# Kernel head of a hybrid mLSTM and gMLP step: four instead of six columns of x turned ahead of the first product, and lower halves made ahead of the next normalisation

## The chip, the cores and the metric

The kernel runs on one core of a Trainium2 chip. The metric is the device time of one execution in microseconds; three runs of the kernel before gave a median of 1468.02 us (1467.85 to 1468.49). The engines are PE (TensorE; its weight loads are listed as PEld), DVE (VectorE), ACT (ScalarE), POOL (GpSimd) and SP (which issues transfers). DMA queue q1 carries the transfers that SP issues, q0 those that POOL issues.

## The reference

One layer. `h = RMSNorm_pre(x)` for 256 prompt rows and 32 sample rows (288 in all), then one product `h @ w_in` whose columns feed two mixers: a chunkwise mLSTM (heads of 256) and a gMLP with a spatial gate. Their outputs are projected, gated and summed, multiplied by `w_out`, normalised and added to x. Only its first steps matter here:

```
h      = x * rsqrt(mean(x*x) + eps) * g_pre
proj   = h @ w_in                      # 2048 x (9 x 2048 + 16 + ...) columns
vb_n   = layernorm(vb)                 # vb: one of the column groups
s      = tril(w_s[g]) @ vb_n + b_s     # spatial gate; w_s is used transposed
y_b    = u * s * silu(zb)
```

## The kernel before

All large products are made in three matmuls. Each operand is split into an upper half (rounded to the fp32r format) and a lower half (the rest): `xh`, `xl` for the normalised x and `whi`, `wlo` for the weights. Then `xh*whi + xl*whi + xh*wlo` is summed (L454, L455, L456). The contraction runs over 16 blocks of 128 rows, k = 0 to 15, and each weight tile ("pair", 256 output columns) comes in four chunks c of four k each. There are 104 pairs; pairs 0 to 7 make `vb`. Per k and pair there are two column halves, so six matmuls of 128x288.

A chunk of weights goes round this ring: SP loads it into `raw` (L394), ACT rounds it into `whi` (L805), DVE subtracts to give `wlo` (L1070), and PE uses both. SP may load the next pair's chunk c into `raw` once DVE has made the lower half of this pair's chunk c. ACT may write `whi` for the next pair's chunk once PE has finished with this pair's.

The head, with all its order written by hand: x is loaded and squared (ACT and DVE), POOL makes the reciprocal root (L1675), and ACT (prompt rows 0 to 127, L830) and DVE (the other rows, L1099) normalise it in quarters of 512 columns, that is four k at a time: `normalise(0)` serves k = 0 to 3, `normalise(1)` k = 4 to 7 and so on. PE turns each k with three transposes (L488, L489: function `turn_x`), ACT writes `xh` from the turned block (L840) and DVE writes `xl` (L1112). Then PE can make the product of that k. Before the first product PE fills time with matmuls nobody reads (L470).

In the head PE turns k = 0 to 5, then goes into the first pair: in front of product k it turns block k + 5 (for k = 1 to 10) and waits for `xl` of k (function `x_piece`). So all 16 blocks are turned when product k = 10 begins. DVE normalises quarter 1 before its first `xl`, and quarters 2 and 3 in front of `xl` of k = 4 and 6.

What hangs on the last turned block (semaphore `x_t` = 16): POOL waits for it (L1683), since the normalised x makes room for its next tiles. It sets a few tiles and then issues four loads of 3 MB together, in this order: `wsn` (the gate weights, L1694), `bsb`, `lng` and `lnb` (L1698). PE turns `wsn` after chunk 0 of pair 1 (L505), DVE masks it into `wsT` (L1200), right behind the lower half of pair 2's chunk 0, and PE reads `wsT` after chunk 2 of pair 1 (L512, function `w_s_corners`):

```
    def w_s_corners():
        pe.wait_ge(ws_set, 2)
        nc.tensor.matmul(ps[:, 6, 0:S], rep4[:], wsT[:, :, 0:TS], start=True, stop=True)...
```

Between pairs 0 and 1 PE makes the gate columns from 32 matmuls (L497, L498) with a small tile `wg2` that ACT and DVE split right after the last `xh` and `xl`; ACT then makes `whi` of pair 1's chunks 0 to 2.

Of the kernel before, what the change touches and what calls it, by code (L numbers as in the profile page):

```python
# [102 lines left out]
def build(nc, x_prompt, x_sample, state_C, state_n, state_m, state_conv, g_pre, w_in, b_ig, b_fg,  # L103
# [258 lines left out]
    def x_bank(k):  # L362
        return 2 + k % 6
# [77 lines left out]
    def _(pe):  # L441
# [26 lines left out]
        def idle_run(n):  # L468
            for _ in range(n):
                nc.tensor.matmul(ps[:, 7, 0:P], ident[:], ident[:], start=True, stop=True)  # L470
# [6 lines left out]
        def turn_x(k0, k1):  # L477

            for k in range(k0, k1):
                if k % 4 == 0:  # L480
                    pe.wait_ge(x_norm_a, k // 4 + 1)
                    pe.wait_ge(x_norm, 2 * (k // 4) + 2)
                if k == 4:
                    pe.wait_ge(par_set, 1)
                if k >= 6:
                    pe.wait_ge(x_lo, k - 5)
                for t in range(2):
                    pe.transpose(ps[:, x_bank(k), P * t:P * t + P], hb0[:, t, P * k:P * k + P], ident[:])  # L488
                pe.transpose(ps[:, x_bank(k), TP:TP + P], hb0[:, 2, P * k:P * k + P],  # L489
                             ident[:]).then_inc(x_t, 1)  # L490
# [47 lines left out]

        def x_piece(k):

            if 1 <= k <= 10:
                turn_x(k + 5, k + 6)
            pe.wait_ge(x_lo, k + 1)

        def v_body(i, first=False, second=False):
            for s in range(2):
                for c in range(CHUNKS):
                    chunk(V0 + s + 2 * i, c, s, None if first else i, xh, xl,
                          x_piece if first and s == 0 else None)
                    if first and (s, c) == (0, 3):  # L550
                        gate_sums()
                    if first and (s, c) == (1, 0):
                        turn_w_s()
                    if c == 1 and not (first and s == 0):
                        if first:
                            pe.wait_ge(g_in, 1)
                        if second and s == 0:
                            pe.wait_ge(ws_set, 3)
                        if not (first or second):
                            pe.wait_ge(g_set, 1)  # L560
                        turn_v(1 - s, 2 * i + s - 1, reused=not (first or second and s == 0))
                    if first and (s, c) == (1, 2):
                        w_s_corners()
                    if second and (s, c) == (1, 3):
                        pe.wait_ge(tok_ev, 3)
                        gates()

        idle_run(11)
        turn_x(0, 6)
        v_body(0, first=True)  # L570
        v_body(1, second=True)
        with pe.Fori(2, 4) as i:
# [493 lines left out]
    def _(dve):  # L1066
        def split_lo(pair, c):

            dve.wait_ge(hi_ready, 4 * pair + c + 1)
            nc.vector.tensor_tensor(wlo[:, c], raw[:, c], whi[:, c].bitcast(F32),  # L1070
                                    ALU.subtract).then_inc(lo_ready, 1)
# [24 lines left out]
        def normalise(q):  # L1096
            for t in (1, 2):
                n = P if t < 2 else S
                nc.vector.tensor_scalar(hb0[0:n, t, QUARTERS[q]], xt[0:n, t, QUARTERS[q]], rstd[0:n, t:t + 1], None,  # L1099
                                        ALU.mult).then_inc(x_norm, 1)  # L1100

        normalise(0)
        split_lo(0, 0)
        normalise(1)
        dve.wait_ge(par_set, 1)
        for k in range(KT):
            if k in (4, 6):
                normalise(k // 2)
            if k in (4, 8, 12):
                split_lo(0, k // CK)  # L1110
            dve.wait_ge(x_hi, k + 1)
            nc.vector.scalar_tensor_tensor(xl[:, k, :], ps[:, x_bank(k), 0:T], par1[:, 32 + k:33 + k],  # L1112
                                           xh[:, k, :].bitcast(F32), ALU.mult, ALU.subtract).then_inc(x_lo, 1)
# [719 lines left out]
```

## Time and profile before

| | us |
|---|---|
| median of three runs | 1468.02 |
| the profiled execution, its own time | 1468.24 |
| its span, first to last instruction | 1465.8 |
| PE busy | 1451.2 (99%) |
| DVE busy | 866.5 (59%) |
| ACT busy | 618.7 (42%) |
| POOL busy | 189.0 (13%) |

The mean granted TensorE clock is 0.997 of full speed. A table of stages of the head, from the view that cuts the span into stretches (busy us of each engine, granted clock, share of the DMA engines):

| stretch, us | PE | DVE | ACT | POOL | clock | DMA |
|---|---|---|---|---|---|---|
| 10 to 13 | 3.00 | 2.38 | 2.51 | 2.04 | 1.00 | 1.09 |
| 16 to 20 | 4.00 | 4.00 | 4.00 | 0.00 | 1.00 | 0.54 |
| 24 to 28 | 4.00 | 2.96 | 2.34 | 0.33 | 1.00 | 0.62 |
| 36 to 44 | 8.00 | 2.60 | 0.99 | 0.00 | 1.00 | 1.02 |
| 44 to 52 | 8.00 | 7.43 | 5.19 | 0.00 | 1.00 | 0.75 |

A busy PE in this table only says that its queue of matmuls never ran dry; how fast it goes is read from the distance between the starts of its matmuls. The engine that waits is found by the bracket behind a row of the timeline, which names the idle time in front of the row and what ended it.

### The profile page before, as it was taken

To read this page: it belongs to the slowest core of one execution; us is meant where nothing else is said; L and a number is where in the kernel's file an instruction comes from. 1 tells how busy PE (TensorE), PEld (TensorE's weight loads), DVE (VectorE), ACT (ScalarE), POOL (GpSimd) and SP (SyncE) were. 2 spreads that over 40 slices of the span, in tenths; PEclk is the share of its full clock that TensorE was granted. 3 is DMA by queue.
4 is the path that set the end of the run, shared out by engine and by line. 5 is a ranking of instruction groups with operands and counts; after the bars stand their busy time and mean duration, and the time that the engine had idled before them with its cause. 6 is when DMAs were issued, how large, how long until landed. Compare 5 with 4: busy or idle time off the path is not lost. (4 is left out here: it accounts for less than half of the span.)

```text
span 1465.8 us, 31006 instructions
## 1 busy us (share of the span) xinstructions
PE 1451.2 (99%) x11100; PEld 1430.1 (98%) x11100; DVE 866.5 (59%) x1433; ACT 618.7 (42%) x870; POOL 189.0 (13%) x340
## 2 busy tenths in 40 slices
PE   9999999999999999999999999999999999999996
PEld 9999999999999999999999999999999999999996
DVE  7766555564434447586767676767667544545444
ACT  6433343343333334454544444545454433333442
POOL 4000000001000000404040414141312000000000
PEclk9999999999999999999999999999999999999998
DMA  7664655557555568696959596979696665555543
GB/s 229 224 160 136 182 162 166 162 151 242 185 172 174 182 185 212 168 298 170 311 161 311 164 303 173 289 185 294 174 295 161 217 180 176 177 178 188 172 159 140
DMA packets 310676, 292.11 MB, mean 199 GB/s; under 512 B 82880, under 2 KB 297608, under 8 KB 309840
## 3 DMA queue, kind: packets, MB, share of 16 engines
q1 hardware_dynamic: 291424, 243.05, 58.4%
q0 software_dynamic: 18960, 48.48, 9.7%
q8 instruction: 23, 0.38, 0.1%
q10 hardware_dynamic: 256, 0.10, 0.0%
q14 instruction: 13, 0.11, 0.0%
HBM read 266.11 MB, written 25.44 MB: 199 GB/s over the span
## 5 line engine op out<-in xcount | busy, mean ns | idle before, releaser
L1070 DVE TENSOR_TENSOR wlo<-raw,whi 128x1024 fp32r<-128x1024 f32 x416 | 506.6, 1222 | 518.2 <-ACT whi L805 516.3
L454 PE MATMUL ps<-xh,whi 128*128 128x288 f32 x2560 | 761.2, 297 | 0.0
L455 PE MATMUL ps<-xl,whi 128*128 128x288 f32 x2560 | 757.6, 296 | 0.0
L456 PE MATMUL ps<-xh,wlo 128*128 128x288 f32 x2560 | 754.6, 295 | 0.0
L805 ACT ACTIVATE whi<-raw 128x1024 fp32r<-128x1024 f32 x416 | 439.3, 1058 | 690.8 <-PE ps L456 655.2
L454 PEld LDWEIGHTS ps<-xh,whi 128*128 128x128 f32 x2560 | 481.7, 188 | 4.8 <-issue 3.3
L455 PEld LDWEIGHTS ps<-xl,whi 128*128 128x128 f32 x2560 | 481.3, 188 | 0.4
L456 PEld LDWEIGHTS ps<-xh,wlo 128*128 128x128 f32 x2560 | 481.0, 188 | 0.0
L455 PE MATMUL ps<-yl,whi 128*128 128x288 f32 x512 | 151.6, 296 | 0.0
L456 PE MATMUL ps<-yh,wlo 128*128 128x288 f32 x512 | 151.0, 295 | 0.0
L454 PE MATMUL ps<-yh,whi 128*128 128x288 f32 x512 | 150.1, 293 | 0.0
L454 PEld LDWEIGHTS ps<-yh,whi 128*128 128x128 f32 x512 | 96.4, 188 | 0.0
L455 PEld LDWEIGHTS ps<-yl,whi 128*128 128x128 f32 x512 | 96.2, 188 | 0.0
L456 PEld LDWEIGHTS ps<-yh,wlo 128*128 128x128 f32 x512 | 96.2, 188 | 0.0
L454 PE MATMUL ps<-mh,whi 128*128 128x288 f32 x248 | 73.5, 297 | 0.0
L455 PE MATMUL ps<-ml,whi 128*128 128x288 f32 x248 | 73.4, 296 | 0.0
L456 PE MATMUL ps<-mh,wlo 128*128 128x288 f32 x248 | 73.1, 295 | 0.0
L1756 POOL DMA_DIRECT2D out_dram<-cst x64 | 36.0, 562 | 229.3 <-DVE cst L1450 224.3
L454 PEld LDWEIGHTS ps<-mh,whi 128*128 128x128 f32 x248 | 46.6, 188 | 0.0
L455 PEld LDWEIGHTS ps<-ml,whi 128*128 128x128 f32 x248 | 46.6, 188 | 0.0
L456 PEld LDWEIGHTS ps<-mh,wlo 128*128 128x128 f32 x248 | 46.6, 188 | 0.0
L1351 DVE SCALAR_TENSOR_TENSOR hb<-xp,par,hb 128x312 f32<-128x312 f32 x96 | 46.3, 537 | 0.0
(348 smaller groups left out, 1014.8 us busy)
## 6 DMA issues: line engine op xcount, KB each, us to landing
raw<-in_w_in_dram SPq DMA_DIRECT2D x320, 512.0 KB, 3.9
raw<-in_w_pb_dram SPq DMA_DIRECT2D x32, 512.0 KB, 3.4
Cin<-in_state_mlstm_C_dram POOLq DMA_DIRECT2D x16, 1024.0 KB, 8.6
Xb<-in_state_mlstm_C_dram SPq DMA_DIRECT2D x256, 64.0 KB, 3.7
out_dram<-Cin POOLq DMA_DIRECT2D x16, 1024.0 KB, 6.3
raw<-in_w_pa_dram SPq DMA_DIRECT2D x32, 512.0 KB, 3.4
raw<-in_w_out_dram SPq DMA_DIRECT2D x32, 512.0 KB, 3.5
bcs<-rows_d POOLq DMA_DIRECT2D x8, 304.0 KB, 3.8
```

What stands on the lines that cost most here:

```text
L454: nc.tensor.matmul(out, whi[:, c, kk, cols], mh_[:, k, :], start=(k == 0), stop=False)
L455: nc.tensor.matmul(out, whi[:, c, kk, cols], ml_[:, k, :], start=False, stop=False)
L456: last = nc.tensor.matmul(out, wlo[:, c, kk, cols], mh_[:, k, :], start=False, stop=(k == KT - 1))
L805: nc.scalar.activation(whi[:, c], raw[:, c], ACT.Copy).then_inc(hi_ready, 1)
L1070: nc.vector.tensor_tensor(wlo[:, c], raw[:, c], whi[:, c].bitcast(F32), ALU.subtract).then_inc(lo_ready, 1)
L1351: ins = nc.vector.scalar_tensor_tensor(out, src, w_at, out, ALU.mult, ALU.add)
L1756: pool.dma_start(blocks_of(conv_p_v, h, s, g), cst[g:g + 3, 2 * s:2 * s + 2, :]).then_inc(cst_out, 16)
```

## The change

On PE, four blocks are turned ahead of the first product. Blocks 4 and 5 are turned in front of product k = 2, and block k + 3 in front of product k for k = 3 to 12. On DVE, `normalise(1)` moves from ahead of the loop to in front of `xl` of k = 2, and quarters 2 and 3 move from k = 4 and 6 to k = 5 and 8. ACT's, POOL's and SP's code is as it was; ACT still normalises quarter 1 ahead of its loop and quarters 2 and 3 at k = 4 and 6.

```diff
         def x_piece(k):
 
-            if 1 <= k <= 10:
-                turn_x(k + 5, k + 6)
+            if k == 2:
+                turn_x(4, 6)
+            if 3 <= k <= 12:
+                turn_x(k + 3, k + 4)
             pe.wait_ge(x_lo, k + 1)
...
         idle_run(11)
-        turn_x(0, 6)
+        turn_x(0, 4)
         v_body(0, first=True)
...
         normalise(0)
         split_lo(0, 0)
-        normalise(1)
         dve.wait_ge(par_set, 1)
         for k in range(KT):
-            if k in (4, 6):
-                normalise(k // 2)
+            if k in (2, 5, 8):
+                normalise((k + 1) // 3)
             if k in (4, 8, 12):
                 split_lo(0, k // CK)
             dve.wait_ge(x_hi, k + 1)
```

Line numbers in the changed kernel are larger by two from `x_piece` on, and by one behind DVE's loop.

First place: PE from the turning of block 3 on. `hb_77` is the normalised x (it shares a place with what lies there later). Before:

```order
L488 MATMUL ps<-ident,hb_77 128x128 x2
L489 MATMUL ps<-ident,hb_77 128x128
L488 MATMUL ps<-ident,hb_77 128x128 x2
L489 MATMUL ps<-ident,hb_77 128x128
L488 MATMUL ps<-ident,hb_77 128x128 x2
L489 MATMUL ps<-ident,hb_77 128x128
L454 MATMUL ps<-xh,whi 128x288
```

Now:

```order
L488 MATMUL ps<-ident,hb_77 128x128 x2
L489 MATMUL ps<-ident,hb_77 128x128
L454 MATMUL ps<-xh,whi 128x288
L455 MATMUL ps<-xl,whi 128x288
L456 MATMUL ps<-xh,wlo 128x288
```

Six transposes have left the place ahead of the first product; twelve matmuls, products k = 0 and 1, now stand ahead of them.

Second place: DVE from `normalise(0)` on. Before:

```order
L1099 TENSOR_SCALAR hb_77<-xt,rstd 128x512
L1099 TENSOR_SCALAR hb_77<-xt,rstd 32x512
L1070 TENSOR_TENSOR wlo<-raw,whi 128x1024
L1099 TENSOR_SCALAR hb_77<-xt,rstd 128x512
L1099 TENSOR_SCALAR hb_77<-xt,rstd 32x512
L1112 SCALAR_TENSOR_TENSOR xl<-ps,par_63,xh 128x288 x4
L1099 TENSOR_SCALAR hb_77<-xt,rstd 128x512
L1099 TENSOR_SCALAR hb_77<-xt,rstd 32x512
L1070 TENSOR_TENSOR wlo<-raw,whi 128x1024
```

Now:

```order
L1101 TENSOR_SCALAR hb_77<-xt,rstd 128x512
L1101 TENSOR_SCALAR hb_77<-xt,rstd 32x512
L1072 TENSOR_TENSOR wlo<-raw,whi 128x1024
L1113 SCALAR_TENSOR_TENSOR xl<-ps,par_63,xh 128x288 x2
L1101 TENSOR_SCALAR hb_77<-xt,rstd 128x512
L1101 TENSOR_SCALAR hb_77<-xt,rstd 32x512
L1113 SCALAR_TENSOR_TENSOR xl<-ps,par_63,xh 128x288 x2
L1072 TENSOR_TENSOR wlo<-raw,whi 128x1024
L1113 SCALAR_TENSOR_TENSOR xl<-ps,par_63,xh 128x288
```

Two `xl` now stand ahead of the pair of instructions that normalises quarter 1, and quarter 2 comes behind the lower half of weight chunk 1.

Third place: PE around the end of the turning, with its waits. Before, behind the last turned block, where product k = 11 has no turn in front of it:

```order
L488 MATMUL ps<-ident,hb_77 128x128 [waits x_lo]
L488 MATMUL ps<-ident,hb_77 128x128
L489 MATMUL ps<-ident,hb_77 128x128
L454 MATMUL ps<-xh,whi 128x288 [waits x_lo]
L455 MATMUL ps<-xl,whi 128x288
L456 MATMUL ps<-xh,wlo 128x288
L454 MATMUL ps<-xh,whi 128x288
L455 MATMUL ps<-xl,whi 128x288
L456 MATMUL ps<-xh,wlo 128x288
L454 MATMUL ps<-xh,whi 128x288 [waits x_lo]
```

Now the last turned block stands in front of product k = 12, the first of weight chunk 3, and waits for that chunk's lower half as well:

```order
L488 MATMUL ps<-ident,hb_77 128x128 [waits x_lo,lo_ready]
L488 MATMUL ps<-ident,hb_77 128x128
L489 MATMUL ps<-ident,hb_77 128x128
L454 MATMUL ps<-xh,whi 128x288 [waits x_lo]
L455 MATMUL ps<-xl,whi 128x288
```

The last turn has moved behind two more products.

## Rows read from the trace of the kernel before

**Rows 1.** The page: PE and its weight loads over the span.

```profile
PE 1451.2 (99%) x11100; PEld 1430.1 (98%) x11100; DVE 866.5 (59%) x1433; ACT 618.7 (42%) x870; POOL 189.0 (13%) x340
```

**Rows 2.** PE's waits over the span: total us, times, longest us.

```profile
PE ps L470 <- POOL ident L1640: 1.8, 1, 1.8
PE ps L744 <- DVE vf_o L1617: 0.6, 1, 0.6
PE ps L488 <- issue: 0.4, 1, 0.4
```

**Rows 3.** Timeline of PE: start us, us, line, tiles, count.

```profile
14.64 0.38 PE L488 MATMUL ps<-ident,hb 128*128 128x128 f32 x2
...
15.51 0.41 PE L488 MATMUL ps<-ident,hb 128*128 128x128 f32 x2 [0.38 <-issue]
...
16.99 0.38 PE L488 MATMUL ps<-ident,hb 128*128 128x128 f32 x2
...
18.12 0.38 PE L488 MATMUL ps<-ident,hb 128*128 128x128 f32 x2
...
27.11 0.38 PE L488 MATMUL ps<-ident,hb 128*128 128x128 f32 x2
...
28.24 0.30 PE L454 MATMUL ps<-xh,whi 128*128 128x288 f32 x1
...
29.03 0.29 PE L454 MATMUL ps<-xh,whi 128*128 128x288 f32 x1
```

**Rows 4.** Timeline of ACT: first and last upper halves of x, then pair 2.

```profile
14.24 1.67 ACT L840 ACTIVATE xh<-ps,par 128x288 fp32r<-128x288 f32 x4 [0.30 <-PE ps L489]
...
27.64 0.50 ACT L840 ACTIVATE xh<-ps,par 128x288 fp32r<-128x288 f32 x1 [0.62 <-PE ps L489]
...
43.01 1.06 ACT L805 ACTIVATE whi<-raw 128x1024 fp32r<-128x1024 f32 x1 [8.87 <-DMA raw<-in_w_in_dram]
```

**Rows 5.** Timeline of DVE from the first lower half of weights.

```profile
13.40 1.21 DVE L1070 TENSOR_TENSOR wlo<-raw,whi 128x1024 fp32r<-128x1024 f32 x1
14.54 0.86 DVE L1099 TENSOR_SCALAR hb<-xt,rstd 128x512 f32<-128x512 f32 x2
15.33 1.77 DVE L1112 SCALAR_TENSOR_TENSOR xl<-ps,par,xh 128x288 fp32r<-128x288 f32 x4
...
28.18 0.52 DVE L1112 SCALAR_TENSOR_TENSOR xl<-ps,par,xh 128x288 fp32r<-128x288 f32 x1 [0.61 <-ACT xh L840]
...
44.10 1.23 DVE L1070 TENSOR_TENSOR wlo<-raw,whi 128x1024 fp32r<-128x1024 f32 x1 [4.62 <-ACT whi L805]
...
45.42 1.29 DVE L1200 TENSOR_TENSOR wsT<-ps,tri 128x512 f32<-128x512 f32 x2
```

**Rows 6.** Timeline of POOL: the wait for the last turned block, and the first load's issue.

```profile
27.67 0.21 POOL L1683 MEMSET rep<- 128x128 f32 x1 [12.55 <-PE ps L489]
...
29.60 0.93 POOL L1694 DMA_DIRECT2D wsn<-in_w_s_dram  x1
```

**Rows 7.** SP's timeline from 28 us; DMA issues, KB each, us to landing.

```profile
30.97 1.50 SPq L394 DMA_DIRECT2D raw<-in_w_in_dram  x2
...
raw<-in_w_in_dram SPq DMA_DIRECT2D x1, 512.0 KB, 12.0
...
lnb<-in_ln_b_dram POOLq DMA_DIRECT2D x1, 1024.0 KB, 11.2
```

**Rows 8.** DMA queues, 38 to 40 us: packets, MB, share of 16 engines.

```profile
q0 software_dynamic: 107, 0.75, 88.3%
q1 hardware_dynamic: 108, 0.11, 15.5%
```

**Rows 9.** PE at the place that reads `wsT`.

```profile
47.41 0.30 PE L512 MATMUL ps<-wsT,rep 128*128 128x32 f32 x2
```

**Rows 10.** Stretches: busy us (and count) per engine, granted clock, DMA share, GB/s.

```profile
1454.00:1456.00 2.00, 0.55 (x3) 0.31 (x3) 1.37 (x6) 0.00 (x0) 0.87 (x1) 1.00 0.00 0
1456.00:1458.00 2.00, 0.00 (x0) 0.00 (x0) 2.00 (x4) 0.00 (x0) 0.00 (x0) 0.79 0.25 61
```

## The prediction, made before the changed kernel ran

> **What bounds the kernel now.** I read the page first: PE and its weight loads are busy for 99% and 98% of the span, DVE for 59% [rows 1]. A busy share does not prove a bound, so I read PE's waits next. There is one at the very start (for the identity), one of 0.4 us inside the head, and the rest belong to the last few microseconds, at L744 and behind [rows 2]; between the head and the last chunk PE waits for nothing. So two things are to be found: how much of the head's wait goes, and whether a new wait appears. Whatever PE loses or gains early is passed on one for one to the end, since nothing behind has a gap to absorb it.
>
> The timeline of PE shows the wait. Blocks are turned 0.33 us apart; block 3 starts at 14.64, so block 4 could start at 14.97, but it starts at 15.51 [rows 3]. The gap between the starts is 0.54 us too long. DVE explains it: its part of quarter 1 ends at 14.54 + 0.86 = 15.40, and PE goes on 0.11 us later [rows 5]. From there on the head runs at PE's pace: a turn and a product take 16.99 to 18.12, that is 1.13 us; a product alone 28.24 to 29.03, that is 0.79 us [rows 3]. The difference is the turn, 0.33 us, so mixing turns between products costs nothing visible.
>
> **The change, part by part.** Work is neither added nor removed: 48 transposes, 16 products, the same instructions on DVE. Only gaps on PE count.
>
> *The first product.* PE is free at 14.97. The first `xh` begins at 14.24 on ACT [rows 4]; one such instruction takes 0.50 us (the last one, alone, at 27.64), so it ends at 14.74. DVE follows 0.04 us later (27.64 + 0.50 = 28.14, and DVE starts at 28.18 [rows 5]), at 14.78; it is free then, since the weight's lower half ends at 13.40 + 1.21 = 14.61. With 0.52 us for `xl` it ends at 15.30, and with the 0.11 us from DVE to PE the first product starts at 15.41. The new gap is 15.41 - 14.97 = 0.44 us in place of 0.54. Gain: 0.10 us. The old wait was for DVE's normalisation, the new one is for the chain transposes, `xh`, `xl`, which hardly ends earlier. From both sides: the gain can't be above the whole 0.54 us, and if each of the two handovers took 0.1 us more the term would be a loss of 0.1. I take 0.10.
>
> *The lookahead.* PE now turns three blocks ahead, not five. Next in line is product 1 at 15.41 + 0.79 = 16.20. Its `xl` starts one DVE step after the first (four take 1.77, one 0.52, so a step is 0.42 [rows 5]): 15.20 + 0.52 + 0.11 = 15.83, 0.37 us in time. Block 4 is turned at 16.99. DVE begins quarter 1 at 14.78 + 2 x 0.42 = 15.62, ends at 16.48, and PE may go at 16.59, 0.40 us in time. I carried the three engines on in this way, with ACT's and DVE's own order and the durations of the same rows: from product 2 on every wait is met at least 0.6 us early, with the closest at products 2, 4, 5 and 8. Cost: nothing. The cover is DVE's speed, since DVE needs about 0.42 us for an `xl` and PE 1.12 for its step; without it each missed block would cost PE its own lateness once.
>
> *What comes late.* The last turn moves. It starts when 12 products and the 11 turns of blocks 4 to 14 are done: 15.41 + 12 x 0.79 + 11 x 0.33 = 28.52 us, against 27.11 before [rows 3], 1.41 us later. Everything that hangs on it moves by as much. POOL wakes at 29.08 in place of 27.67, and the first of its four loads is issued at 31.01 in place of 29.60 [rows 6]. The last `xh` moves from 27.64 to 29.05 [rows 4], the last `xl` from 28.18 to 29.59; behind them in ACT's and DVE's order stand the gate columns and the halves of pair 1. So the first lower half of pair 1 comes 1.41 us later, and with it SP's load of pair 2's chunk 0, from 30.97 to 32.38 [rows 7].
>
> The gate columns and pair 1 itself are still in time: PE comes to the gate columns at 28.52 + 0.33 + 4 x 0.79 = 32.01 us and to pair 1 behind their 32 matmuls, while DVE is through with the last `xl` at 30.1 and with pair 1's chunk 0 by 32.38. The load for pair 2 is another matter. It takes 12.0 us, since POOL's 3 MB are in flight beside it and the last of them takes 11.2 [rows 7]; from 38 to 40 us POOL's queue moves 0.75 MB and SP's 0.11 [rows 8]. Both queues start 1.41 us later, so I move the landing by the same: ACT, which waited 8.87 us for it, starts at 44.42 in place of 43.01 [rows 4]. DVE waits for ACT and moves from 44.10 to 45.51, and behind that lower half stand the two instructions that make `wsT`: they end at 45.42 + 1.29 = 46.71 before, and at 48.12 now [rows 5].
>
> PE reads `wsT` at 47.41 [rows 9], 0.10 earlier now, at 47.31. Before, it could have gone at 46.71 + 0.11 = 46.82, so there was only 0.59 us of room. Now it may go at 48.12 + 0.11 = 48.23. A new wait of 0.92 us. Behind the waiting instruction are chunk 3 of pair 1 and everything after. The bounds of this wait: zero, if the landing moves by under half a microsecond; 1.5 us, if it moves by another 0.6. I take 0.92, since the handovers around it are all fixed by single rows.
>
> *Sum.* -0.10 + 0.92 = +0.82 us. The profiled execution took 1468.24 us, of which 1465.8 is the span and 2.4 lies around it, and would take 1469.06. It stands 0.22 us above the median of the runs, so by the median I forecast 1468.02 + 0.82 = 1468.84, say 1468.8. PE has no gap behind this place [rows 2], so its delay stays and no new one follows; pair 2's first product, one chunk of 4 x 0.79 us behind the place that reads `wsT`, finds its chunk ready (45.51 + 1.23 = 46.74).
>
> 0.2% of this time is 2.9 us, about what a measurement can tell from no change. So the forecast is that no change can be told.
>
> **Rivals.** *A: no new wait.* The loads land no more than half a microsecond later, for instance because the DMA engines idle before 31 us and catch up. For it: nothing in the trace fixes the landing of one queue when both are moved. Against it: the two queues together fill the engines (88.3% and 15.5% [rows 8]), so there is nothing to catch up with. Time: 1468.02 - 0.10 = 1467.92. A smaller gap in front of the first product belongs here; at most 0.54 is there, so 1467.5 is the floor.
>
> *B: the shorter lookahead starves PE.* If ACT's or DVE's handovers are 0.4 us slower than I carried them, products 1 and 2 wait for DVE. The margins of 0.37 and 0.40 us speak against it; each miss costs only the amount by which it exceeds the margin. Together with the wait at `wsT`, which grows by what comes late and shrinks by what PE has lost, perhaps 0.5 us more: 1469.3.
>
> *C: the clock falls, and the kernel is slower beyond doubt.* The new wait is longer than any in PE's middle. The granted clock is still 1.00 from 1454 to 1456 us, where PE is busy for 0.55 us of 2; it falls, to a mean of 0.79, in the next stretch, in which PE does nothing at all [rows 10]. If the wait at 47.3 us brought the level of 1.2 GHz in place of 2.4, each microsecond spent there would lose half a microsecond; it decides from some 4.2 us at half speed on, which with the 0.82 make 2.9 us. With 6 us it is 1468.8 + 3 = 1471.8. Against it stands that a full stretch with a quarter of work did not bring the fall. The Trainium skill ("TensorE: Matmul & The Clock Gate", Part 1: The HAM clock gate) says that a hardware monitor lets the clock through by how busy the array has been lately; by that rule this change, which adds idle time on PE, could pay twice, while by the rows it pays once. The trace agrees that idleness is followed by a fall, and shows none behind a wait of the size that I expect.
>
> **How the numbers follow.** The forecast's own case, a wait of 0.4 to 1.5 us at `wsT`: 0.62, from 1468.3 to 1469.4. Rival A: 0.26. Rival B: 0.08. Rival C: 0.03. The remaining 0.01 is a gain that I do not see. Range: from 1467.6 (A, with some scatter of the median: the three runs spread over 0.64 us) to 1469.6 (the own case with the upper bound of the wait, and most of B). All but C and the last case lie within 0.2%, also with some scatter between chips: same 0.94, slower 0.04, faster 0.02.
>
> **What would show it.** In the timeline of PE: the first product at 15.4 us, behind a gap of 0.4; turns of blocks 4 and 5 at about 17.0 without a wait; no other gap up to 36 us; the last turn at 28.5. POOL's wait ending at 29.1. ACT's first half of pair 2 at 44.4 in place of 43.0. A wait of PE at L512, not there before, for DVE's `wsT`, 0.9 us long, after which PE's rows run 0.8 us later than before up to the end. If the landing has not moved, the wait is missing and rival A holds; if PE waits in front of products 1 to 8 for `xl`, it is B; a clock under 1.00 around 48 us is C. A difference of over 2.9 us without one of these would mean that something far from the head depends on it, which I have argued it does not.

## The result and the profile after

The changed kernel took 1469.20 us (median of 22 runs, 1468.69 to 1471.65) against 1467.86 us (22 runs, 1467.12 to 1468.53). The ratio is 1.0012, 95% interval 1.0006 to 1.0017: slower, by 1.3 us in the medians, clear of noise and inside 0.2%. The profiled execution took 1469.09 us, its span is 1467.5 us, and it lies on the median of the 22 spans.

PE's waits over the span, in the changed kernel (total us, times, longest us):

```profile
PE ps L470 <- POOL ident L1641: 1.8, 1, 1.8
PE ps L512 <- DVE wsT L1201: 1.0, 1, 1.0
PE ps L746 <- DVE vf_o L1618: 0.7, 1, 0.7
PE ps L454 <- DVE xl L1113: 0.4, 1, 0.4
```

Against [rows 2], the wait in front of block 4 (L488) has become one of the same size in front of the first product (L454, for `xl`), and a new wait of 1.0 us stands at L512, for `wsT`. Where they lie shows the timeline of PE:

```profile
14.07 0.41 PE L488 MATMUL ps<-ident,hb 128*128 128x128 f32 x2
...
15.08 0.38 PE L488 MATMUL ps<-ident,hb 128*128 128x128 f32 x2
...
15.97 0.37 PE L454 MATMUL ps<-xh,whi 128*128 128x288 f32 x1 [0.40 <-DVE xl L1113]
...
17.63 0.38 PE L488 MATMUL ps<-ident,hb 128*128 128x128 f32 x2
...
29.21 0.38 PE L488 MATMUL ps<-ident,hb 128*128 128x128 f32 x2
...
49.03 0.41 PE L512 MATMUL ps<-wsT,rep 128*128 128x32 f32 x2 [0.96 <-DVE wsT L1201]
```

No other wait stands between. This execution began its turns at 14.07 us, 0.45 us later than the profiled one of before; that comes from the load of x and has no part in the change (ACT begins to square x at 7.08 us here). So everything below is counted from the first turn: 13.62 us in the kernel before, 14.07 here. The chain behind the new wait, on ACT, DVE and POOL:

```profile
14.69 1.68 ACT L842 ACTIVATE xh<-ps,par 128x288 fp32r<-128x288 f32 x4 [0.30 <-PE ps L489]
...
45.28 1.06 ACT L807 ACTIVATE whi<-raw 128x1024 fp32r<-128x1024 f32 x1 [10.25 <-DMA raw<-in_w_in_dram]
```

```profile
15.31 0.94 DVE L1113 SCALAR_TENSOR_TENSOR xl<-ps,par,xh 128x288 fp32r<-128x288 f32 x2 [0.25 <-ACT xh L842]
...
46.37 1.23 DVE L1072 TENSOR_TENSOR wlo<-raw,whi 128x1024 fp32r<-128x1024 f32 x1 [6.38 <-ACT whi L807]
...
47.69 1.29 DVE L1201 TENSOR_TENSOR wsT<-ps,tri 128x512 f32<-128x512 f32 x2
```

```profile
29.76 0.21 POOL L1684 MEMSET rep<- 128x128 f32 x1 [14.43 <-PE ps L489]
...
31.48 0.25 POOL L1691 TENSOR_SCALAR_AFFINE_SELECT blk<-blk 32x32 f32<-32x32 f32 x1
31.70 0.94 POOL L1695 DMA_DIRECT2D wsn<-in_w_s_dram  x1
```

The links of the forecast are all there. The last turn is 29.21 - 14.07 = 15.14 us behind the first, against 13.49 [rows 3]. POOL's first load is issued at +17.63 against +15.98 [rows 6], ACT finds pair 2's load at +31.21 against +29.39 [rows 4], DVE ends `wsT` at 48.98, and PE reads it at +34.96 against +33.79 [rows 9].

All kernels of this study in the same measure, from their timelines. "Pair 2's load used" is the start of ACT's first instruction on it. "Last matmul" is the start of the last row of L769 in the kernel before (1453.24 us there) and of the same instruction in the others. Spans are medians over the runs; on the chips of the experiments the kernel before had 1465.8 or 1465.9.

| us from PE's first turn | first product | last turn | POOL's first load | pair 2's load used | L512 | wait there | last matmul | median span |
|---|---|---|---|---|---|---|---|---|
| before | 2.49 | 13.49 | 15.98 | 29.39 | 33.79 | none | 1439.62 | 1465.9 |
| before, late lng and lnb | 2.43 | 13.44 | 15.93 | 26.21 | 33.73 | none | 1439.84 | 1465.8 |
| changed | 1.90 | 15.14 | 17.63 | 31.21 | 34.96 | 0.96 | 1440.91 | 1467.5 |
| changed, second look | 1.90 | 15.16 | 17.64 | 30.87 | 34.63 | 0.61 | 1440.58 | 1467.4 |
| changed, late lng and lnb | 1.87 | 15.11 | 17.60 | 26.30 | 33.82 | none | 1439.68 | 1466.1 |
| changed, L512 one chunk later | 1.91 | 15.15 | 17.63 | 31.42 | 37.02 | none | 1439.68 | 1465.9 |
| changed, POOL's loads first | 1.87 | 15.11 | 15.90 | 29.13 | 33.81 | none | 1439.65 | 1466.2 |
| changed, catching up | 1.90 | 13.54 | 16.03 | 29.64 | 33.83 | none | 1439.66 | 1466.1 |
| PE's part alone | 2.12 | 15.36 | 17.85 | 31.09 | 34.84 | 0.62 | 1441.45 | 1467.6 |
| DVE's part alone | 3.65 | 14.66 | 17.15 | 30.82 | 34.95 | none | 1441.63 | 1467.3 |
| before, POOL late, first dose | 2.27 | 13.27 | 19.36 | 26.04 | 39.12 | none, 3.80 at L505 | 1444.98 | 1470.6 |
| before, POOL late, second dose | 2.28 | 13.29 | 19.38 | 26.06 | 37.46 | none, 3.66 at L505 | 1444.15 | 1470.9 |
| before, half a lower half first | 1.95 | 12.95 | 15.44 | 25.73 | 33.25 | none | 1439.08 | 1465.6 |
| before, half a lower half first, fewer fillers | 1.95 | 12.95 | 15.44 | 25.72 | 33.25 | none | 1439.07 | 1465.4 |

### The profile page after: what moved, and what is told of

Read it like the earlier page. It is cut to its first block and busy times, and to the rows that moved or that the text cites. A ratio compares the mean times of both kernels' runs of the same rounds, so it can differ in the third digit from the quotient of the medians.

```text
span 1467.5 us, 31006 instructions
## 1 busy us (share of the span) xinstructions
PE 1451.9 (99%) x11100; PEld 1430.5 (97%) x11100; DVE 866.9 (59%) x1433; ACT 619.0 (42%) x870; POOL 188.8 (13%) x340
## 5 line engine op out<-in xcount | busy, mean ns | idle before, releaser
L454 PE MATMUL ps<-xh,whi 128*128 128x288 f32 x2560 | 761.3, 297 | 0.4 <-DVE xl L1113 0.4
L454 PEld LDWEIGHTS ps<-xh,whi 128*128 128x128 f32 x2560 | 481.7, 188 | 5.4 <-issue 3.5
L454 PE MATMUL ps<-yh,whi 128*128 128x288 f32 x512 | 150.1, 293 | 0.0
L454 PEld LDWEIGHTS ps<-yh,whi 128*128 128x128 f32 x512 | 96.3, 188 | 0.0
L454 PE MATMUL ps<-mh,whi 128*128 128x288 f32 x248 | 73.6, 297 | 0.0
L454 PEld LDWEIGHTS ps<-mh,whi 128*128 128x128 f32 x248 | 46.6, 188 | 0.0
```

The lines of the kernel that those rows point to most:

```text
L454: nc.tensor.matmul(out, whi[:, c, kk, cols], mh_[:, k, :], start=(k == 0), stop=False)
```

## The experiments

Two theories were set against each other. W: the loss is PE's wait at L512, at the end of the chain last turn, POOL's loads, pair 2's load, `wsT`. H: it is made in the head itself.

**The large loads late.** In the changed kernel:

```diff
+        pool.wait_ge(ws_t, 1)
         pool.dma_start(lng[:], ln_g.partition_broadcast(P)).then_inc(ln_in, 16)
```

> The changed kernel, but POOL issues the two large loads lng and lnb only after PE has turned wsn (ws_t = 1), so they no longer stand beside SP's load of pair 2. Theory W (the lost time is PE's wait at L512 for wsT, which waits for pair 2's load behind POOL's 3 MB): the load lands by 40 us in place of 45, the wait of 0.96 us at L512 is gone, and the time falls to 1467.9 us, within 0.3 us of the kernel before (ratio 0.9999 to 1.0002). Rival H (the time is lost in the head itself, in front of the first products, and by a later start of the head): the wait at L512 may go, but the time stays at 1469 us or above (ratio 1.0008 or more).

Measured: 1467.83 us against 1467.59, ratio 1.0001 (0.9992 to 1.001). PE does not wait at L512, and ACT now waits for PE, not for the load:

```profile
40.35 1.06 ACT L807 ACTIVATE whi<-raw 128x1024 fp32r<-128x1024 f32 x1 [5.37 <-PE ps L456]
```

W holds. Of the 1.3 us, PE's last matmul has got back 1440.91 - 1439.68 = 1.23, and 0.06 against the kernel before is left.

**The reader late.** In the changed kernel, with no load touched:

```diff
-                    if first and (s, c) == (1, 2):
+                    if first and (s, c) == (1, 3):
                         w_s_corners()
...
-        v_body(0, {(0, 1, 0): (), (0, 3): (gates_a,), (1, 0): (w_s_masked,), (1, 2): (w_s_blocks,)})
+        v_body(0, {(0, 1, 0): (), (0, 3): (gates_a,), (1, 0): (w_s_masked,), (1, 3): (w_s_blocks,)})
```

> The changed kernel, but PE reads wsT behind chunk 3 of pair 1 in place of chunk 2, 3.2 us later, and DVE makes its tile from it one chunk later too. No load is touched. Theory W: pair 2's load still lands near 45 us, but PE does not wait at L512 any more; 1467.9 us (ratio 0.9999 to 1.0002). Rival H: 1469 us or above. If this one is fast and e1_lng_late is not, the late lng and lnb cost something of their own.

Measured: 1468.26 us, ratio 1.0004 (0.9995 to 1.0013), above what W expected, with the interval holding both. The profile decides: the load lands as late as in the changed kernel and `wsT` ends at 48.65 us, but PE comes for it at 50.55 and passes:

```profile
50.55 0.30 PE L512 MATMUL ps<-wsT,rep 128*128 128x32 f32 x2
```

The median span is 1465.9 us, that of the kernel before. The difference in the medians lies outside the span: 2.36 us in the median here, 1.59 in the kernel before on the same chip. Run by run this part is about 1.6 us in most executions and 1.8 to 3.6 us in the others, in the kernel before as in the changed one, so of 11 runs the spans tell more than the times.

**The control.** The kernel before with the same late `lng` and `lnb`.

> The kernel before with the same late lng and lnb as e1_lng_late: a control, since it has no wait at L512. Theory W: no change, 1467.9 us (ratio 0.9998 to 1.0002). If it becomes faster by 0.3 us or more, PE was losing to the transfers in some way that its waits do not show, and e1's gain would not be the wait at L512 alone.

Measured: 1467.56 us, ratio 0.9998 (0.9989 to 1.0007), median span 1465.8. As expected: without a wait at L512 the late loads bring nothing. (A wait of 0.3 us at L621 stands in its last matmul's 1439.84.)

**POOL late in the kernel before, in two doses.** The first:

```diff
         pool.wait_ge(x_t, KT)
+        pool.wait_ge(gw_lo, 2)
```

> The kernel before, but POOL's block behind the last turned block also waits for the gate columns' lower halves (gw_lo = 2), so that its loads are issued about 1.5 us later, while PE's, ACT's and DVE's head and SP's load of pair 2 stay where they were. Theory W in the form that the end of POOL's loads sets the landing of pair 2's load: that landing moves by 1.2 to 1.6 us, PE waits 0.8 to 1.0 us at L512, 1468.8 us (ratio 1.0005 to 1.0008). If SP's own issue time sets it, the landing moves by less than 0.6 us, there is no wait and the ratio is 0.9999 to 1.0002.

Measured: 1472.58 us, ratio 1.0031 (1.0019 to 1.0043). A miss: over five times the loss I expected, and at another place. The first row is PE's, the rest is POOL's timeline:

```profile
43.46 1.09 PE L505 MATMUL ps<-ident,wsn 128*128 128x128 f32 x8 [3.80 <-DMA bsb<-in_b_s_dram]
```

```profile
29.90 0.12 POOL L1688 MEMSET blk<- 32x32 f32 x1
30.09 0.69 POOL L1656 TENSOR_SCALAR_AFFINE_SELECT tri<-tri 128x128 f32<-128x128 f32 x1
30.85 1.07 POOL L1656 TENSOR_SCALAR_AFFINE_SELECT blk<-blk 32x32 f32<-32x32 f32 x1
31.99 1.13 POOL L1691 TENSOR_SCALAR_AFFINE_SELECT blk<-blk 32x32 f32<-32x32 f32 x1
33.08 0.94 POOL L1695 DMA_DIRECT2D wsn<-in_w_s_dram  x1
```

POOL's wait ended 1.4 us later, as meant, but its first load was issued at 33.08, 3.5 us later. Three small operations, which the changed kernel's POOL does in 0.40, 0.20 and 0.25 us, took 0.69, 1.07 and 1.13. SP's load, issued at 30.85, was now 2.2 us ahead of POOL's, not 1.4 behind. Its first chunk landed 3.5 us after its issue, and `bsb`, which PE needs at L505, came at 43.4.

The wait of 3.8 us is not the whole loss. Behind it the granted clock fell to 0.50, the level of 1.2 GHz, with PE busy throughout:

```profile
44.00:45.00 1.00, 1.00 (x10) 1.00 (x8) 0.39 (x2) 0.00 (x0) 0.00 (x0) 0.90 1.05 415
45.00:48.00 3.00, 3.00 (x14) 3.00 (x14) 1.06 (x2) 0.00 (x0) 0.00 (x0) 0.50 0.99 388
```

From L505 to L512 PE takes 39.12 - 29.74 = 9.38 us in place of 33.79 - 26.01 = 7.78, so the low clock cost 1.6 us on top. Five of the six executions have a mean granted clock of 0.995 and spans of 1470.5 us or more; the sixth has 0.996 and 1468.6. The second dose waits for the last `xl`:

```diff
         pool.wait_ge(x_t, KT)
+        pool.wait_ge(x_lo, KT)
```

> The kernel before, with POOL's block waiting for the last xl (x_lo = 16) in place of the last turned block, 1.0 to 1.1 us later; a smaller dose than e4_before_pool_late. If POOL's small operations are stretched by DVE's subtractions of pair 1, which begin at 29.5 us, its first load is issued at 32.5 to 33.1 us in place of 29.6, SP's load for pair 2 goes first, and PE waits 2.5 to 4 us for bsb at L505: 1470.5 to 1472 us. If the delay is passed on as it is (1.1 us), PE waits nowhere or at L512 for under 0.8 us and the time is 1467.5 to 1468.3.

Measured: 1472.45 us, ratio 1.003 (1.0021 to 1.004), a wait of 3.7 us at L505. In this profile the clock stayed at 1.00 behind it, and a wait of 0.8 us at L621 adds to the loss; of the ten executions the seven with a mean clock of 0.994 or 0.995 have spans of 1470.3 to 1472.3, the other three 1469.0 to 1470.6. With a wait that ended at 28.80 us, 0.3 us sooner than in the first dose, the first load was issued at 33.18, no sooner:

```profile
29.59 0.12 POOL L1688 MEMSET blk<- 32x32 f32 x1
29.78 1.09 POOL L1656 TENSOR_SCALAR_AFFINE_SELECT tri<-tri 128x128 f32<-128x128 f32 x1
30.94 1.07 POOL L1656 TENSOR_SCALAR_AFFINE_SELECT blk<-blk 32x32 f32<-32x32 f32 x1
32.08 1.13 POOL L1691 TENSOR_SCALAR_AFFINE_SELECT blk<-blk 32x32 f32<-32x32 f32 x1
33.18 0.93 POOL L1695 DMA_DIRECT2D wsn<-in_w_s_dram  x1
```

So the delay isn't passed on as it is. It pushes POOL's operations beside DVE's subtractions of pair 1, here in the second dose, and between the wait's end and the first issue POOL takes 3.98 and 4.38 us in place of 1.93, 2.0 and 2.4 us more:

```profile
29.50 3.60 DVE L1070 TENSOR_TENSOR wlo<-raw,whi 128x1024 fp32r<-128x1024 f32 x3 [0.41 <-ACT whi L805]
```

The changed kernel escapes this only because its last turn delays DVE's subtractions too, which start at 31.62, when POOL's operations are nearly done. The kernel with POOL's loads first, below, shows it a third time: it runs the same three operations later, beside the subtractions, and they take 0.58, 1.08 and 1.13 us. No run takes the subtractions away and leaves the rest, so the cause rests on these three profiles; in the second dose each of the three operations ends 0.06 to 0.14 us behind the end of a subtraction.

**PE's part alone.** The kernel before with the first two hunks of the change, and DVE in its old order.

> PE's part of the change alone: four turns ahead, DVE in the order of the kernel before (quarter 1 normalised ahead of the first xl). Theory W, with the durations seen: the first xl starts only behind quarter 1, so PE's gap in front of the first product is 0.9 to 1.0 us in place of 0.54 in the kernel before and 0.5 in the changed one; the last turn starts 2.0 to 2.1 us later than in the kernel before, counted from PE's first turn (1.65 in the changed kernel); the wait at L512 is 1.0 to 1.4 us. 1469.3 us, ratio to before 1.0010 to 1.0014. Rival H (DVE's order and the lookahead make the loss, not the late last turn): less than 0.5 us slower.

Measured: 1469.23 us, ratio 1.0011 (1.0002 to 1.002).

```profile
PE ps L454 <- DVE xl L1114: 0.6, 1, 0.6
PE ps L512 <- DVE wsT L1202: 0.6, 1, 0.6
PE ps L623 <- DVE Yb L1362: 0.6, 1, 0.6
```

The first product starts at +2.12, not at the +2.35 or so that I expected, and the last turn is 1.87 later than in the kernel before, not 2.0. This execution's fillers ended late, so its turns began 0.24 us behind the point where the normalised x was ready, and that much of the gap was hidden. The wait at L512 is smaller than I said, 0.6 us. The third wait, at L623 inside the mLSTM stage, shows in four profiles of this study (0.3 to 0.8 us) and not in the others; it doesn't go with the change.

**DVE's part alone.** The kernel before with the last hunk, PE turning six.

> DVE's part alone: quarter 1 normalised behind two xl, while PE still turns six blocks ahead and keeps its lookahead of five. PE waits for quarter 1 in front of block 4: gap 1.5 to 1.7 us in place of 0.54. The last turn stands where it stood in PE's order, so PE and POOL's loads are late together and theory W has no wait at L512: the loss is the longer gap alone, 1.0 to 1.1 us, 1468.6 us, ratio 1.0006 to 1.0008. If a wait at L512 shows all the same, the landing of pair 2's load does not follow the last turn as W has it.

Measured: 1468.83 us, ratio 1.0008 (0.9999 to 1.0017). PE's gap in front of block 4, and the place that reads `wsT`:

```profile
16.65 0.41 PE L488 MATMUL ps<-ident,hb 128*128 128x128 f32 x2 [1.55 <-issue]
...
48.55 0.30 PE L512 MATMUL ps<-wsT,rep 128*128 128x32 f32 x2
```

The first product is 3.65 - 2.49 = 1.16 us later, L512 34.95 - 33.79 = 1.16, and there is no wait: here the last turn is 1.17 us late and PE 1.16, so PE is as late as what it waits for (the load is found 1.43 us later, which leaves some of the 0.59 us of room). That separates the two ways to be late. What hurts at L512 is not a late last turn but one that is late against PE's own work. (A wait of 0.8 us at L621 makes up the rest of its last matmul's 2.01.)

**Catching up.** The changed kernel, but the lookahead is rebuilt at once:

```diff
             if k == 2:
-                turn_x(4, 6)
-            if 3 <= k <= 12:
-                turn_x(k + 3, k + 4)
+                turn_x(4, 7)
+            if k == 3:
+                turn_x(7, 9)
+            if 4 <= k <= 10:
+                turn_x(k + 5, k + 6)
...
-            if k in (2, 5, 8):
-                normalise((k + 1) // 3)
+            if k in (2, 4, 6):
+                normalise(k // 2)
```

> The changed kernel with its four turns and two xl ahead, but PE catches up at once: three turns in front of product 2, two in front of 3, then block k + 5 as before, and DVE normalises quarters 2 and 3 at k = 4 and 6 again. So the last turn stands in front of product 10 as in the kernel before. Theory W: the last turn comes within 0.15 us of the kernel before (counted from PE's first turn), pair 2's load lands as before, no wait at L512, 1467.6 us (ratio 0.9999 to 1.0002): the loss of the changed kernel is gone with the first product still early. Rival H: the loss of 1.3 us stays for the most part (1468.6 or more).

Measured: 1468.28 us, ratio 1.0004 (0.9995 to 1.0013), median span 1466.1. The last turn is back at +13.54 and pair 2's load at +29.64; the wait is gone and PE's last matmul stands at 1439.66, with the first product as early as in the changed kernel. So H, a loss made in the head itself, does not hold. The median is higher than W expected. Its part outside the span is 1.71 us in the median. The median span is 0.3 us above that of the kernel before on the same chip; the profile, 0.2 above the kernel before's, began its turns 0.18 us later and shows no wait of PE to go with the rest, so it stays open.

**The changed kernel again.**

> The changed kernel once more, unaltered, beside the kernel before on one chip: a second profile, to see how much the wait at L512 varies. Theory W: PE waits at L512 again, for 0.8 to 1.4 us; pair 2's load is used by ACT 31.0 to 31.6 us after PE's first turn (29.4 in the kernel before); ratio to before 1.0008 to 1.0012, median span 1.3 to 1.7 us longer. If the wait is gone in this profile while the time is the same, something else carries the loss.

Measured: 1469.03 us, ratio 1.001 (1.0001 to 1.0019).

```profile
48.38 0.41 PE L512 MATMUL ps<-wsT,rep 128*128 128x32 f32 x2 [0.61 <-DVE wsT L1201]
```

The same wait, 0.35 us shorter, below the band I gave, since the load was found at +30.87 in place of +31.21.

**POOL's loads first.** The changed kernel with the four `dma_start` of `wsn`, `bsb`, `lng` and `lnb` moved right behind POOL's wait:

```diff
         pool.wait_ge(x_t, KT)
+        pool.dma_start(wsn[:], ...)
+        pool.dma_start(bsb[:]...)
+        pool.dma_start(lng[:], ...)
+        pool.dma_start(lnb[:], ...)
         nc.gpsimd.memset(rep4[:], 0.0)
```

> The changed kernel, but POOL issues its four loads ahead of its small operations, 1.9 us earlier. Theory W with the landing following POOL's issue: ACT uses pair 2's load 29.2 to 29.8 us after PE's first turn in place of 31.2, no wait at L512, a span within 0.3 us of the kernel before (ratio 0.9999 to 1.0003). If the landing follows SP's issue instead, it stays at 31.2 and so does the wait.

Measured: 1467.86 us, ratio 1.0001 (0.9991 to 1.001).

```profile
43.23 1.06 ACT L807 ACTIVATE whi<-raw 128x1024 fp32r<-128x1024 f32 x1 [8.20 <-DMA raw<-in_w_in_dram]
```

POOL's first load is 1.73 us earlier (+15.90 for +17.63), SP's load is issued where it was (33.07 us in both profiles), and ACT finds pair 2's load 2.08 us earlier, at +29.13. So the landing follows POOL's issue: SP's load now takes 10.1 us in place of 12.2. In the eight profiles in which POOL's 3 MB go first, ACT uses pair 2's load 13.2 to 13.8 us behind POOL's first issue.

**A head without the gap.** From the kernel before: late `lng` and `lnb`, and the lower half of pair 0's chunk 0 in two pieces.

```diff
         normalise(0)
-        split_lo(0, 0)
+        dve.wait_ge(hi_ready, 1)
+        nc.vector.tensor_tensor(wlo[:, 0, 0:2], ...).then_inc(lo_first, 1)
         normalise(1)
         dve.wait_ge(par_set, 1)
         for k in range(KT):
+            if k == 2:
+                nc.vector.tensor_tensor(wlo[:, 0, 2:4], ...).then_inc(lo_ready, 1)
```

PE waits for `lo_first` in front of product 0 and for `lo_ready` in front of product 2.

> The kernel before with lng and lnb late, and the lower half of pair 0's chunk 0 made in two pieces: two k ahead of quarter 1's normalisation, two behind the second xl. Quarter 1 is then ready 0.55 us earlier and PE's turns and first product follow each other without the gap of 0.54 us. Expected: no wait of PE in the head, first product 1.98 to 2.05 us after the first turn in place of 2.49, time 0.4 to 0.5 us under the kernel before, 1467.1 us, ratio 0.9996 to 0.9998. If the gap only moves (to xl of k = 0 or to the second piece), the time stays at 1467.6.

Measured: 1467.40 us against 1467.46, ratio 0.9998 (0.9989 to 1.0007). The profile shows what was expected: no wait of PE in the head, first product at +1.95, last matmul 1439.08, 0.54 us under the kernel before. The time hardly shows it, since the 11 runs spread from 1466.54 to 1469.04. The next version also runs 7 in place of 11 fillers ahead of the first turn (`idle_run(7)`).

> e7_first_half_lo with 7 in place of 11 of the filler matmuls (L470's line) between the parameters' transposes and the first turn. In three profiles the fillers ended late and held the first turn back by up to 0.24 us. Expected: the first turn 1.01 to 1.03 us behind the start of DVE's normalisation in this profile, the granted clock still 1.00, and a span 0.3 to 0.6 us under the kernel before. If the idle time in front of the first turn costs clock, the granted clock falls under 1.00 between 13 and 20 us and the time is over 1468.

Measured: 1466.96 us (1466.79 to 1467.14) against 1467.55, ratio 0.9995 (0.9986 to 1.0004). The stretches of this kernel (busy us per engine, clock, DMA share, GB/s):

```profile
13.00:16.00 3.00, 2.30 (x20) 2.28 (x21) 3.00 (x8) 2.77 (x7) 2.23 (x4) 1.00 1.10 302
16.00:20.00 4.00, 4.00 (x34) 4.00 (x33) 4.00 (x8) 4.00 (x8) 0.00 (x0) 1.00 0.59 175
```

The clock stays at the level of 2.4 GHz though PE had waited 1.8 us in front of the first turn. All 11 spans lie between 1465.2 and 1465.5 us; the kernel before spreads from 1465.7 to 1466.5 beside it. It is the fastest kernel here by its median, and all its spans lie under all those of the kernel before, though the interval of the ratio does not clear 1. The fillers themselves were a source of scatter: where they begin late, they hold the first turn back, by 0.53 us in the profile with POOL's loads first, whose turns begin 1.55 us behind DVE's normalisation and not 1.02.

## Why the prediction was wrong

It named +0.82 us as the sum and went from there to "no change can be told", because 0.2%, 2.9 us, would be about what a measurement can tell. That step failed first: the interval of the ratio, 1.0006 to 1.0017, is 0.8 us wide to either side, so a loss of the size that its own sum gave is told. The other steps that failed are two terms of the sum: the gain of 0.10 us in front of the first product, which is a loss of 0.05, and the fixed landing behind the wait of 0.92 us, which varies and costs 0.89 and 1.24 us with what follows it. The mechanism, its place and the sign of the sum were right, and the time is within the range.

*The first product.* Forecast: 1.79 us behind the first turn, a gain of 0.10. Measured: 1.90 in both profiles, and the turns of blocks 4 and 5 bring no wait. The handovers failed, the step for which I took 0.04 and 0.11 us from rows of other pairs. Here DVE starts 15.31 - (14.69 + 0.50) = 0.12 us behind ACT, and PE 15.97 - (15.31 + 0.52) = 0.14 us behind the end of `xl`. The forecast had 0.04 and 0.11; the two differences, 0.08 and 0.03, are the 0.11 us by which the product came late. The first two products then took 17.63 - 15.97 = 1.66 in place of 1.58 us. By L505 PE stands at +26.06, against 26.01 before: the term is a loss of 0.05, a gain of 0.10 was forecast. Both bounds of that term held it.

*The lookahead.* Cost nothing, as said: no wait of PE between the first product and L512.

*The last turn.* Forecast 1.41 us later, measured 1.65 (15.14 - 13.49): the 0.11 and 0.08 us of the step above, and small change.

*The wait at L512.* Forecast 0.92 us. Against PE's own work before it, L512 is late by 34.96 - 33.79 - 0.05 = 1.12 us in one profile and by 34.63 - 33.79 - 0.07 = 0.77 in the other. The chain is shown from both ends: take the large loads away, issue them earlier, or restore the last turn, and the wait goes; move the reader alone, with the load as late as ever, and it goes too. What I had wrong was to take the landing as a fixed shift. The first profile found the load 1.82 us later than the kernel before did, the second 1.48, for a forecast of 1.41 and a last turn 1.65 and 1.67 us later; behind POOL's first issue it varies by 0.56 us over eight profiles. Before, 0.59 us of room swallowed that; now all of it reaches PE.

*Left out: the restart.* Behind the wait PE's next product starts 49.28 - 49.03 = 0.25 us after L512 (0.24 in the second profile); before it was 47.55 - 47.41 = 0.14. With 0.01 or 0.02 more that makes 0.12 us at the last matmul, in both profiles.

*Sum.* At PE's last matmul +1.29 and +0.96 us in the two profiles, which is 0.05 + 1.12 + 0.12 and 0.07 + 0.77 + 0.12: up to there nothing is missing. The medians of the spans differ by 1.5 to 1.6, and the profiles show where the rest lies in these two executions. The first, 1.7 us longer than the profile before, began its turns 0.45 us later. The second, 1.5 us longer, began them 0.13 us later and lost 0.34 us behind the matmul of the table, since the granted clock fell while PE still had transposes to make (first row: its stretch from 1455 us, clock 0.69; then its transposes, and those of the first profile):

```profile
1455.00:1456.00 1.00, 0.67 (x3) 0.50 (x3) 0.41 (x4) 0.00 (x0) 0.50 (x1) 0.69 0.00 0
1455.33 0.69 PE L746 MATMUL ps<-ident,vf_o 128*128 128x128 f32 x2 [0.64 <-DVE vf_o L1618]
1455.99 0.44 PE L746 MATMUL ps<-ident,vf_o 128*128 128x128 f32 x2 [0.65 <-DVE vf_o L1618]
```

Neither belongs to the change: the control, which has no wait at L512, shows the same slow transposes (0.68 us) and a first turn 0.21 us later, with a span of 1466.6 us. So 0.96 to 1.29 us of the change are shown. The shortest span of the second look, 1466.7 us, is 1.0 us over the shortest of the kernel before on the same chip. Whether the rest of the 1.5 us between the medians is longer waits at L512 or such scatter stays open; the spans of the changed kernel reach up to 1469.1 us, and both profiles are of executions near the median.

*The rivals.* A (the landing does not move) is refuted by all profiles of the changed kernel. B (the lookahead starves PE) does not occur. C (the clock falls) does not occur in the changed kernel: around the wait of 0.96 us the granted clock is 1.00. Its mechanism exists, though: in the first dose above it came behind a wait of 3.8 us and cost 1.6.

```profile
48.00:52.00 4.00, 3.04 (x23) 2.97 (x23) 3.94 (x8) 2.69 (x4) 0.00 (x0) 1.00 0.69 186
```

One rival was missing: that a later POOL runs into DVE's subtractions. With all three operations beside them POOL's loads fall behind SP's, and the whole is worth 5 us, the low clock of most of those executions included. In the changed kernel the last of the three begins at 31.48 us and the subtractions at 31.62.

## What to carry to other kernels

A change at the front of a kernel is judged by what hangs on its last event, not on its first. Here the first product came 0.59 us earlier and the last turn 1.65 us later, and the room of a wait three transfers away (0.59 us) decided the time. Before a step is moved, work out the room at each place that waits for its end, and take the scatter of the transfers out of that room first.

## What the hardware showed that I had not expected

POOL's operations that read the on-chip memory stall beside DVE's two-operand subtractions. An AFFINE_SELECT of 32x32 takes 0.20 or 0.25 us alone and 1.07 to 1.13 beside them, about one subtraction; a MEMSET of the same tile takes 0.11 alone and 0.12 beside (at 29.59 us in the second dose, where the first subtraction runs since 29.50), 0.15 in the kernel with POOL's loads first. The Trainium skill ("SBUF — State Buffer", SBUF: two separate sides) says that a DVE operation with two SBUF inputs locks the port pair it shares with GpSimd, but only against a GpSimd operation that reads SBUF, and for the whole instruction. The trace agrees: the operation that reads is held until a subtraction ends, and the MEMSET, which only writes, is hardly touched (0.01 to 0.04 us).

Two queues on the same DMA engines don't share by what is asked of them. Issued 1.4 us behind POOL's first load, SP's half megabyte for pair 2 lands 11.8 to 12.4 us after its issue (seven profiles); issued 2.2 us ahead, it lands after 3.5, and POOL's half megabyte `bsb` takes 9.4 us in place of 5.6. They come nearer to sharing by packets: in the 2 us of [rows 8] they moved 107 and 108 of them, which are 0.75 and 0.11 MB, since POOL's are seven times as large. The changed kernel's profile has 108 and 107 from 40 to 42 us, that of POOL's loads first 107 and 103 from 38 to 40; other stretches are less even (77 and 107 in the changed kernel from 38 to 40). So a delay of 1 to 2 us in one issue can exchange which transfer is late.
